# First attention of a two-block float32 transformer kernel: probabilities times values in two TensorE passes instead of three, with the halves of the output added by VectorE

## The reference, cut to what matters

```
s = einsum('bnqkgd,bnskd->bnkgqs', q, kb) * HD**-0.5
logits = where(mask, s + bias, NEG)
m = maximum(max(logits, -1), sink)
p = exp(logits - m)
probs = p / (sum(p, -1) + exp(sink - m))
o = einsum('bnkgqs,bnskd->bnqkgd', probs, vb)
h = h + o.reshape(B, T, 1024) @ w_o
```

## Time and profile before

| | us |
|---|---|
| median of 3 runs | 2238.18 |
| lowest, highest | 2234.59, 2249.25 |
| the profiled execution's own time | 2233.79 |
| its span | 2232.0 |
| PE busy | 2084.4 (93%) |
| PEld busy | 1704.2 (76%) |
| DVE busy | 1320.6 (59%) |
| ACT busy | 756.4 (34%) |
| mean granted TensorE clock | 0.971 |

### The profile page before, as it was taken

The page is one execution under the profiler, slowest core; times in us unless marked ns, Lnnn a source line. Parts: engine busy times, 40 slices in busy tenths (PEclk is TensorE's granted clock), DMA queues, the critical chain, the costliest instruction groups (busy, mean ns, idle before and its releaser), DMA issues. The chain is left out here.

```text
span 2232.0 us, 25925 instructions
## 1 busy us (share of the span) xinstructions
PE 2084.4 (93%) x10208; PEld 1704.2 (76%) x10208; DVE 1320.6 (59%) x2243; ACT 756.4 (34%) x1419; POOL 193.9 (9%) x170
## 2 busy tenths in 40 slices
PE   5999888999999999999989999799998999999796
PEld 4777666888888888888668888587877777888685
DVE  6277666752562472464578888775344436777634
ACT  4166343421220220232441212362224235455422
POOL 2032220100000000000020000000001002223201
PEclk9999999999999999999989999899999999999898
DMA  3102001221231231231201122115121210111212
GB/s 139 48 29 86 20 20 55 102 108 48 104 104 48 104 105 55 85 123 48 113 29 38 62 85 62 43 57 194 39 105 60 64 60 29 36 36 38 100 48 85
DMA packets 42872, 156.93 MB, mean 70 GB/s; under 512 B 4352, under 2 KB 9088, under 8 KB 41472
## 3 DMA queue, kind: packets, MB, share of 16 engines
q1 hardware_dynamic: 40304, 146.49, 19.4%
q10 hardware_dynamic: 2448, 8.79, 1.0%
HBM read 135.34 MB, written 19.92 MB: 70 GB/s over the span
## 5 line engine op out<-in xcount | busy, mean ns | idle before, releaser
L173 PE MATMUL banks<-u2H,wH 128*128 128x512 f32 x736 | 297.9, 405 | 15.3 <-DVE u2L L367 4.8
L174 PE MATMUL banks<-u2L,wH 128*128 128x512 f32 x736 | 289.7, 394 | 0.0
L175 PE MATMUL banks<-u2H,wL 128*128 128x512 f32 x736 | 289.3, 393 | 0.0
L173 PE MATMUL banks<-aH,wH 128*128 128x512 f32 x640 | 254.4, 397 | 23.7 <-DVE hm L1046 22.2
L175 PE MATMUL banks<-aH,wL 128*128 128x512 f32 x640 | 251.4, 393 | 0.0
L174 PE MATMUL banks<-aL,wH 128*128 128x512 f32 x640 | 251.3, 393 | 0.0
L168 DVE TENSOR_TENSOR wL<-raw,wH 128x1024 fp32r<-128x1024 f32 x153 | 186.6, 1221 | 90.0 <-ACT wH L163 90.0
L163 ACT CAST wH<-raw 128x1024 fp32r<-128x1024 f32 x153 | 159.7, 1045 | 230.8 <-DMA raw<-in_wstream 226.0
L173 PE MATMUL banks<-mH,wH 128*128 128x512 f32 x512 | 200.2, 391 | 0.6 <-DVE mL L369 0.6
L174 PE MATMUL banks<-mL,wH 128*128 128x512 f32 x512 | 199.9, 390 | 0.0
L175 PE MATMUL banks<-mH,wL 128*128 128x512 f32 x512 | 199.9, 390 | 0.0
(11 more groups left out here) (291 smaller groups left out, 4013.0 us busy)
## 6 DMA issues: line engine op xcount, KB each, us to landing
raw<-in_wstream SPq DMA_DIRECT2D x153, 512.0 KB, 3.6
mod_w<-in_mod_w SPq DMA_DIRECT2D x48, 512.0 KB, 5.3
x_scratch<-h SPq DMA_DIRECT2D x2, 4096.0 KB, 11.8
gt<-gates_scratch SPq DMA_DIRECT2D x8, 640.0 KB, 4.1
h<-in_x SPq DMA_DIRECT2D x4, 1024.0 KB, 10.6
hm<-in_x SPq DMA_DIRECT2D x1, 4096.0 KB, 13.6
h<-x_scratch SPq DMA_DIRECT2D x1, 4096.0 KB, 12.1
xo<-x_scratch SPq DMA_DIRECT2D x1, 4096.0 KB, 12.1
```

The source lines that it names most:

```text
L173: first = pe.matmul(out, aH, bH, start=start, stop=False)
L174: pe.matmul(out, aH, bL, start=False, stop=False)
L175: return first, pe.matmul(out, aL, bH, start=False, stop=stop)
```

## The change

The values of one key-value head now have both their halves in one stationary operand of 128 columns: `vz1a` holds the high part of head 0 beside its low part, `vz1b` the same for head 1, each 3 x 64 columns wide per block with a part of 64 zeros. The first pass takes high and low part together against the tile's high part; the second takes the high part with zeros beside it against the tile's low part. That is two matmuls of 512 columns for each tile where there were three. The output of each key-value head now has its own bank, with one half of the sum on the head's own 64 partitions and the other on the other 64. ScalarE copies the other halves to the right partitions of a new buffer `other1` (`shift`, 2 copies of 64x512), VectorE adds the halves in the bank to it (`add_out`, 2 additions of 64x512), and `out_high` and `out_low` read `other1`. `out_low` moves behind `low` in VectorE's slot, `out_high` behind `tile_high` in ScalarE's. Since the output takes two banks, the ring of the scores goes from three to two. The second attention goes on as before, but that its addition writes into `other` and no longer waits for `o_lo` and for the gate's load. Semaphores of the zeroing and of the return of x are merged.

```diff
-        vz1H = sb("vz1H", [NB, 3 * 64], RX + 8 * KB, F32R)
-        vz1L = sb("vz1L", [NB, 3 * 64], RX + 14 * KB, F32R)
+        vz1a = sb("vz1a", [NB, 3 * 64], RX + 8 * KB, F32R)
+        vz1b = sb("vz1b", [NB, 3 * 64], RX + 14 * KB, F32R)
+        other1 = sb("other1", [TN], RX + 28 * KB)
...
             def o_half(k, kv):
-                return banks[:, O_BANK + k % 2, 256 * kv:256 * kv + 256]
+                if gate:
+                    return banks[:, O_BANK + k % 2, 256 * kv:256 * kv + 256]
+                return banks[:, O_BANK + kv, :]
...
                         if x == 0 and not gate and k >= 1:
-                            pe.wait_ge(o_lo, k)
+                            pe.wait_ge(added, k)
                         pe.wait_ge(p_lo, g + 1)
                         tH, tL = pT[g % nslots]
                         for y, (kv, c0, c1) in enumerate(mults):
                             f = slice(64 * kv, 64 * kv + P)
...
-                            _, m = mm3(pe, o_bank(k), vzH[:, vb, f], vzL[:, vb, f], tH[:, c0:c1], tL[:, c0:c1],
-                                       x == 0 and y == 0, x == len(t_tiles(steps[k])) - 1 and y == len(mults) - 1)
+                            tiles = [z for z, tile in enumerate(t_tiles(steps[k])) if gate or tile[3][0][0] == kv]
+                            pe.matmul(o_half(k, kv), (vza, vzb)[kv][:, vb, 64 * (1 - kv):64 * (1 - kv) + P], tH[:, c0:c1],
+                                      start=x == tiles[0] and y == 0, stop=False)
+                            m = pe.matmul(o_half(k, kv), (vza, vzb)[kv][:, vb, f], tL[:, c0:c1], start=False,
+                                          stop=x == tiles[-1] and y == len(mults) - 1)
...
+                    def add_out(k):
+
+                        dve.wait_ge(shifted, k + 1)
+                        for kv in range(2):
+                            mine = slice(64 * kv, 64 * kv + 64)
+                            m = dve.tensor_tensor(other[mine], o_half(k, kv)[mine].rearrange("p (c q) -> p c q", q=P), other[mine],
+                                                  ALU.add)
+                        m.then_inc(added, 1)
...
+                        if done is not None:
+                            add_out(done)
                         if done is not None and gate:
                             gate_out(done)
-                        elif done is not None:
-                            out_low(dve, done)
                         for tile in slot.turns:
                             low(*tile)
+                        if done is not None and not gate:
+                            out_low(dve, done)
...
                     def shift(k):
                         act.wait_ge(pv_done, tidx[k + 1])
                         if k >= 1:
-                            act.wait_ge(added, k)
+                            act.wait_ge(gated or o_lo, k)
                         for kv in range(2):
-                            mine, other = slice(64 * kv, 64 * kv + 64), slice(64 * (1 - kv), 64 * (1 - kv) + 64)
-                            m = act.copy(gate["other"][mine], o_half(k, kv)[other].rearrange("p (c q) -> p c q", q=P))
+                            mine, there = slice(64 * kv, 64 * kv + 64), slice(64 * (1 - kv), 64 * (1 - kv) + 64)
+                            m = act.copy(other[mine], o_half(k, kv)[there].rearrange("p (c q) -> p c q", q=P))
                         m.then_inc(shifted, 1)
 
                     def out_high(k):
-                        if gate:
-                            act.wait_ge(gated, k + 1)
-                        else:
-                            act.wait_ge(pv_done, tidx[k + 1])
+                        act.wait_ge(gated or added, k + 1)
                         act.copy(o_dst(QH, k), o_src(k)).then_inc(o_hi, 1)
...
-                        if finished(i) is not None and gate:
+                        if finished(i) is not None:
                             shift(finished(i))
-                        elif finished(i) is not None:
-                            out_high(finished(i))
                         for tile in slot.turns:
                             tile_high(*tile)
-                        if finished(i) is not None and gate:
+                        if finished(i) is not None:
                             out_high(finished(i))
...
-                        factor=lambda st: CG_FACTOR if st[1] else 1.0, rings=(3, 3, 5, (3, 4)))
+                        factor=lambda st: CG_FACTOR if st[1] else 1.0, rings=(2, 2, 4, (2, 3)), other=other1[:].rearrange("p (c q) -> p c q", q=P))
```

More of the change, by code:

```diff
@@ L565, in _, with mixed_attention @@
                 linear(pe, W0["qkv"], 6, TILES1, hl(uH, uL), qkv_done, qkv_drained, norm1)
-        def mixed_attention(name, steps, X, pairs, t_tiles, chunks, heads, W, QH, QL, KH, KL, vzH, vzL, in1, sink_of, logits,
-                            pT, vsrc, vblocks, bulk, pace, gate=None, chain_max=False, zeroed=None, waits=(), out_lows=None,
-                            q_ready=None, factor=lambda st: 1.0, rings=(2, 2, 4, (2, 3, 4))):
+        def mixed_attention(name, steps, X, pairs, t_tiles, chunks, heads, W, QH, QL, KH, KL, vza, vzb, in1, sink_of, logits,
+                            pT, vsrc, vblocks, bulk, pace, gate=None, chain_max=False, zero=None, cleared=False, waits=(), out_lows=None,
+                            q_ready=None, factor=lambda st: 1.0, other=None, rings=(2, 2, 4, (2, 3, 4))):
             T_RING = 2
@@ L585, in mixed_attention @@
             o_lo = out_lows or sem(name + "_o_lo")
-            vz_zero = zeroed or sem(name + "_vz_zero")
-            gated, shifted, added = (sem(name + "_" + v) for v in ("gated", "shifted", "added")) if gate else (None,) * 3
+            shifted, added = sem(name + "_shifted"), sem(name + "_added")
+            gated = sem(name + "_gated") if gate else None
             N, nslots = len(steps), len(pT)
@@ L634, in o_half @@
             def o_half(k, kv):
-                return banks[:, O_BANK + k % 2, 256 * kv:256 * kv + 256]
+                if gate:
+                    return banks[:, O_BANK + k % 2, 256 * kv:256 * kv + 256]
+                return banks[:, O_BANK + kv, :]
             def v_high(kv, b, n):
-                return (vzH, vzL)[kv][:, b:b + n, 64:P] if gate else vzH[:, b:b + n, P * kv:P * kv + 64]
+                return (vza, vzb)[kv][:, b:b + n, 64:P]
             def v_low(kv, b, n):
[L644 to L648, removed]
+                return (vza, vzb)[kv][:, b:b + n, P * (1 - kv):P * (1 - kv) + 64]
             def o_src(k):
-                return gate["tmp"] if gate else o_bank(k).rearrange("p (c q) -> p c q", q=P)
+                return gate["tmp"] if gate else other
             def o_dst(a, k):
```

58 lines of the change are left out of this document (22 added, 36 removed).

## The result

The changed kernel takes 2263.93 us, the median of 6 runs (2260.76 to 2267.12); the kernel before, measured with it, takes 2237.88 us (2234.59 to 2249.25). The ratio is 1.0109, with an interval of 1.0094 to 1.0125: slower by 1.1%. The profiled spans are 2258.9 and 2232.0 us, 26.9 us apart. The forecast was 2253, with a range of 2234 to 2268: its direction and its range were right. Its number was 11 us too low. Of these, 4 come from the execution on which I built the sum, which was faster than the median; as a change I had forecast 16.6 + 3 = 19.6 us, and it is 26 to 27, so the change was too small by some 7. That puts the ratio just outside the "within 1%" to which I gave most of the chance. The interval reaches down to 1.0094, so on which side of 1% the change lies the measurement hardly tells.

What follows compares the result with a forecast made beforehand. TensorE bounds the kernel, but this stage only in its first third; elsewhere a VectorE and ScalarE loop without slack does. 2233.8 + 16.6 (5.8 + 8.1 + 2.7) + 3 for the clock = 2253 us, range 2234 to 2268.

Steps and rivals of the forecast that it cites:

- within 1%: Whole kernel: measured time within 1% (22 us) of before, likeliest slower by less than 1%; chance 0.66.
- What bounds the kernel: First attention: a loop over VectorE and ScalarE without slack sets the step, 11.30 us before and 13.3 after.
- The prices: New operations of the first attention: copies 0.58 us each, additions 0.69 each; four hand-overs at the end some 4.1.
- The ring: Scores' two banks cost nothing; only the slot after the first `weigh` could wait, up to 1 us.
- Stretch 1: First attention to 219 us: the longer loop and step k=0, less 0.8 at the last `weigh`, +5.8 us.
- The first output: Step k=0, finished in an x=1 slot: `out_high` waits for the additions ahead of the next exponentials, 1.9 us.
- The six steps: Stretch to 219 us: with the longer loop they take 77.5 us instead of 72.8, 4.7 more.
- Stretch 2: 219 to 342 us, slots that wait for `hm`: plain step +0.5 us, some outputs and slots dearer, sum +8.1.
- the clock: TensorE at half clock after longer waits: two more stretches, +3 us; bounds 0 and five, 8 us.
- my sum without the clock: Whole change before any clock loss: 5.8 + 8.1 + 2.7 = 16.6 us slower.
- The end: Tiles 20 to 31 wait for the last output: some 4.1 us instead of 1.41, +2.7.
- The third rival: Clock falls in most longer waits: five to eight more low stretches of 1.5 us, 2260 to 2268; chance 0.2.

Runs made afterwards that it cites:

- the first two experiments: Kernel before without weigh's low-by-high product: 2228.77 us, ratio 0.9956; changed kernel with a third pass put back, the second one issued twice: 2273.13 us, ratio 1.0162.
- The last experiment: Changed kernel with ScalarE's projection work ahead of `out_high` (ScalarE's other order) in the x=1 slots: single run, span 2255.5 us.
- the one kept busy behind it: Changed kernel with TensorE passes that nobody reads in three slots near the first attention's end: 2262.75 us, ratio 1.0096.
- the one before with early work: Kernel before with the last slot's projection work on VectorE and ScalarE done at the start of the next slot: 2214.59 us, ratio 0.9891.

## Why the prediction was right, and what was mis-sized

**What bounds the kernel: right.** The loop over VectorE and ScalarE has no slack for what the change puts into it. Predicted 13.3 us for it, measured 13.45; the first two experiments split the change into -10 and +36, and with the waits for `hm` away the cost of 23 us stays.

**The prices: right.** 0.581 and 0.689 us; 4.11 us at the end, where I had 4.1; waits for `hm` 33.8 us ("over 30") and for the low parts 15.1 ("over 15"); 120 passes of `weigh`. Only the attention's end, 367.7 us instead of "about 360", is as late as the whole was mis-sized.

**The ring: right.** It costs nothing. The sign that I had named against this, a wait of the scores for a bank, did come, once and 0.9 us long, in the slot where I had allowed up to 1 us; the kernel before with the smaller ring alone has it too and loses nothing.

**Stretch 1: mechanism right, size too small.** +9.1 where I had +5.8. Three parts make it up, by the starts of VectorE's logits. The first output, up to the logits at 145.47 (141.23 before), cost 4.2 where I had 1.9. The last experiment takes 2.2 off that: I let `out_high` wait, but didn't count the projection's operations in ScalarE's queue behind it (1.3), and the rest is the half clock that moved into the next block. The six steps took 78.7 us where I had 77.5, each 0.15 to 0.4 longer: in the step shown, `low` starts at 8.93 us and not at 8.8. And TensorE got back 1.0 where I had 0.8. At the end of the stretch 1.4 of the 3.3 us are the queue's, by the last experiment; the rest is in the steps and the clock, and no run separates these.

**Stretch 2: right but for the clock.** +10.2 from the end of stretch 1 to the last scores, where I had 5.9. The changed kernel has 17 us at half clock there (233, 247, 271 and 281 us), the one before 6.8: up to 5.1 us of loss. Two other experiments have the changed kernel's work in this stretch and other amounts of half clock, the one kept busy behind it and the one with ScalarE's other order:

```
kernel                     length   at half clock
ScalarE's other order       96.5        13.6
changed kernel              98.4        17.1
kept busy behind it        100.4        23.0
before                      88.2         6.8
```

A us at half clock costs 0.34 to 0.54 us there. Carried on to the 6.8 us of the kernel before, the changed one would take 3.5 to 5.1 less (the upper end goes by 0.5, the most that a us at half clock can cost), an estimate from three single traces; it covers the 4.3 that I had too little, and leaves the 5.9 for the loop and the outputs. So my sum without the clock came out here, as a whole; its terms were not tested one by one.

**The end: the chain right, its clock missed.** 4.1 us came as predicted, but after it the dense run to the second norm takes 39.4 us instead of 36.5.

**The clock is the mis-sized term.** I took two more stretches, 3 us, with a bound of 8; there are six more, and by the account above they cost some 7 (4.3 + 2.9), so that the bound, not my value, was near. Stretch 1 brings the other 3.3. The price of a stretch was right (1.5 us; with TensorE kept busy, 5.6 us for 13.6 at half clock). What was wrong was the count. I expected four more waits of 3 us or over, and that half of them would bring such a stretch. The attention's timeline has ten of them, at 142, 202, 236, 247, 272, 282, 324, 340, 350 and 368 us, where the kernel before had two, and all but the one at 324 us (3.29) are followed by passes at half clock; its waits of 2.36 and 2.80 us are not. I had argued that waits of 1.9 us left the clock alone, and hadn't asked what becomes of them when they get 1.4 to 2 us longer. The length of a wait doesn't decide it alone: the wait of 3.29 us at this place was followed by half clock in three of the other kernels (at 326, 328 and 332 us), and one of 1.87 us in the kernel before was too. The rule that I cited in the prediction (the Trainium skill, TensorE: Matmul & The Clock Gate, What's actually happening) says that the throttled state is the default and that activity releases it. The trace agrees for nine of the ten long waits, and its cost of some 7 us is nearer to the 8 that I had worked out by it than to my 3.

**The chances.** The third rival, the clock in most of the longer waits, is what happened: six more stretches, where it had five to eight. Its 2260 to 2268 holds both the median and the profiled execution, partly by luck, since 3.3 us of the excess come from stretch 1 and not from its mechanism. The sign that I had named for it, a mean clock well under 0.91 over the whole stage, did not come: the mean was 0.93, and the sign was badly chosen, for the 0.91 belonged to the lowest part of a stage that had 0.97.

## What to carry to other kernels

Before taking work off the engine with the largest share, follow one step around: if the step is a loop over other engines with a wait in it, saved work there becomes waiting, and what is put between two links of the loop lengthens every step by the part that nothing hides, here 2 us a step for 0.9 us of matmul saved. When a change lengthens waits of TensorE that lie just short of those that already drop its clock, count nearly all of them as drops (here nine of ten waits of 3 us or over). And a wait added ahead of other work in an engine's queue costs what is caught behind it as well. The reverse holds too: the projection's operations on VectorE and ScalarE, moved ahead of the long link, gave the kernel before 1.1%, as much as the change lost.

## What the runs showed that I had not expected

The clock also fell, in some executions, before the first attention begins: at 103 to 105 us of the spans of four of these kernels, which put the whole attention 4 to 6 us later. Behind the attention the clock differs too. From the second norm to the end, where all thirteen kernels do nearly the same work, their traces take 1848.5 us (the one without copies, 100 us at half clock) to 1861.8 (the one before with early work, 126 us). So that last kernel is 28.0 us ahead of the one before at the second norm and 18.3 at the end. Single spans of this kernel are therefore worth no more than some 10 us, and lengths between two places of the program say more, if the time at half clock is read beside them.

A pass that is hidden in a loop is not hidden everywhere in the same stage: the third pass cost 2.2 us in the attention's first 95 us and 9.6 in its last 120, some 3.5 of these by way of the clock.
